# Expert rows fetched by row number, slot weights applied to results, and seven steps moved in a layer-stack kernel

## The reference

```
swiglu:  (silu(h @ w_gate) * (h @ w_up)) @ w_down          # ffn, w 1024x2816 and 2816x1024
mamba2:  y = ssd_chunked(...) + d_skip * xs ; g = y * silu(z)
         g = g * rsqrt(mean(g*g over a group of 256) + eps) * norm_w ; out = g @ w_out   # 8 groups
moe:     h = modulate(rms_norm(x), shift, scale)
         logits = h @ w_router + b ; a group of 4 experts is chosen, and two experts inside it
         out[t] = sum over 2 of weight[t, c] * (silu(h[t] @ w_gate[e]) * (h[t] @ w_up[e])) @ w_down[e]
         x = x + gate * out ; result = rms_norm(x) * norm_final
```

## Time and profile before

| | |
|---|---|
| median of 3 runs | 2996.58 us |
| the profiled execution | 2992.48 us, span 2991.2 us, mean granted TensorE clock 0.952 |
| PE (TensorE) busy | 2768.0 us, 93% |
| PEld (weight loads, beside PE) | 2222.6 us, 74% |
| DVE (VectorE) | 1613.2 us, 54% |
| ACT (ScalarE) | 727.7 us, 24% |
| POOL (GpSimd) | 775.2 us, 26% |
| DMA | 347.21 MB in 491364 packets, mean 116 GB/s |

### The profile page before, as it was taken

One profiled execution on the slowest core, in us unless ns is written; L12 is line 12 of the kernel. 1 busy time (PEld: TensorE's weight loads), 2 busy tenths in 40 slices (PEclk: granted clock), 3 DMA queues, 4 the chain that ended last, 5 costly groups with the idle time before them and its releaser, 6 DMA issues. The chain is left out here.

```text
span 2991.2 us, 32772 instructions
## 1 busy us (share of the span) xinstructions
PE 2768.0 (93%) x12795; PEld 2222.6 (74%) x12795; DVE 1613.2 (54%) x2319; ACT 727.7 (24%) x1336; POOL 775.2 (26%) x804
## 2 busy tenths in 40 slices
PE   5999999999899999999999699899999799858994
PEld 3888887777678888888888599788888576646663
DVE  3434468887743433564455366555454453445766
ACT  2101125555411001110011255210010343322323
POOL 1211121111112111221112288321112033133543
PEclk9999999999999999999999899999999896869997
DMA  3434432222133333354454200154444340149996
GB/s 105 144 112 137 130 92 71 67 68 64 50 87 97 97 94 99 92 148 136 118 147 132 63 1 1 53 147 138 120 141 92 45 63 15 35 141 314 380 377 228
DMA packets 491364, 347.21 MB, mean 116 GB/s; under 512 B 34430, under 2 KB 463307, under 8 KB 490955
## 3 DMA queue, kind: packets, MB, share of 16 engines
q1 hardware_dynamic: 451840, 270.05, 31.5%
q10 hardware_dynamic: 37066, 66.68, 6.4%
q0 software_dynamic: 2304, 8.39, 0.8%
HBM read 314.66 MB, written 30.41 MB: 115 GB/s over the span
## 5 line engine op out<-in xcount | busy, mean ns | idle before, releaser
L225 POOL TENSOR_SCALAR w_hi<-w_lo_exact 128x1024 fp32r<-128x1024 f32 x369 | 405.8, 1100 | 1798.9 <-DMA w_lo_exact<-in_ffn_w_gate 427.6
L240 PE MATMUL bank<-h_hi,w_hi 128*128 128x512 f32 x1992 | 795.9, 400 | 47.9 <-DVE h_lo L311 18.5
L241 PE MATMUL bank<-h_lo,w_hi 128*128 128x512 f32 x1992 | 782.4, 393 | 0.0
L242 PE MATMUL bank<-h_hi,w_lo 128*128 128x512 f32 x1992 | 781.8, 392 | 0.0
L232 DVE TENSOR_TENSOR w_lo<-w_lo_exact,w_hi 128x1024 fp32r<-128x1024 f32 x369 | 453.9, 1232 | 159.4 <-POOL w_hi L225 158.5
L240 PEld LDWEIGHTS bank<-h_hi,w_hi 128*128 128x128 f32 x1992 | 378.2, 190 | 144.5 <-issue 23.3
L242 PEld LDWEIGHTS bank<-h_hi,w_lo 128*128 128x128 f32 x1992 | 378.0, 190 | 80.7
L241 PEld LDWEIGHTS bank<-h_lo,w_hi 128*128 128x128 f32 x1992 | 378.5, 190 | 79.5 <-issue 3.6
L242 PE MATMUL bank<-g_hi,w_lo 128*128 128x512 f32 x704 | 280.9, 399 | 0.0
L241 PE MATMUL bank<-g_lo,w_hi 128*128 128x512 f32 x704 | 277.5, 394 | 0.0
L240 PE MATMUL bank<-g_hi,w_hi 128*128 128x512 f32 x704 | 276.1, 392 | 0.0
(11 more groups left out here) (458 smaller groups left out, 3742.7 us busy)
## 6 DMA issues: line engine op xcount, KB each, us to landing
w_lo_exact<-in_ffn_w_gate SPq DMA_DIRECT2D x88, 512.0 KB, 3.8
w_lo_exact<-in_ffn_w_up SPq DMA_DIRECT2D x88, 512.0 KB, 3.9
w_lo_exact<-in_ssm_w_in SPq DMA_DIRECT2D x48, 512.0 KB, 3.9
mod_w<-in_w_mod ACTq DMA_DIRECT2D x48, 512.0 KB, 3.8
e_lo_exact<-in_w_gate SPq DMA_DIRECT2D x92, 256.0 KB, 7.2
e_lo_exact<-in_w_up SPq DMA_DIRECT2D x92, 256.0 KB, 8.7
e_lo_exact<-in_w_down SPq DMA_DIRECT2D x46, 512.0 KB, 9.9
w_lo_exact<-in_ffn_w_down SPq DMA_DIRECT2D x32, 512.0 KB, 4.0
```

Of the source, the lines that this page charges most:

```text
L225: ge.tensor_scalar(k.w_hi[:, u % SLOTS, :], k.raw[:, u % SLOTS, :], 1.0, 0.0, ALU.mult, ALU.add).then_inc(*k.up("w hi", u))
L240: te.matmul(k.bank[bank][:, :], hi, x_hi, start=first, stop=False)
L241: te.matmul(k.bank[bank][:, :], hi, x_lo, start=False, stop=False)
L242: return te.matmul(k.bank[bank][:, :], lo, x_hi, start=False, stop=stop)
```

## The change

1. `rows_in` becomes an array of the 512 tokens' h rows, stored by four plain stores. The zero stores, the zero tile and the eight scatters go. For each of the 23 blocks a list of token numbers is computed: two one-hot tiles (`row_one`: the row within the block; `block_token`: the block, times the token's number) and eight matmuls. GpSimd gathers each block's rows by its list (`moe_rows_pool`), in place of the plain loads. An empty slot has token number 0.
2. The two weights of a token are brought to slots the same way (`slot_weight`) and multiplied in when `yo` is copied. At the end four gathers bring the first row of each token and four gathers that add bring the second; the two multiplications there go.
3. A gate/up unit holds rows 8p+2i and 8p+2i+1 of partition p: runs of 2 KB. The h columns are dealt to match when they are copied.
4. `norm_vector` scales tile n before it finishes tile n-1 (mixer and experts).
5. Expert stage's head: logits and the turning back of h run tile by tile as the norm makes them; GpSimd's first 12 splits wait for the norm's end; the loads of the router's bias and of the final norm come before the norm; `overflow_vector` comes after the lists.
6. The small loads of setup move to `ffn00`, half 1, j = 1.
7. In Mamba-2 the gate sum moves to unit s = 5 behind its sixth piece, and the last group's output blocks are dealt 8, 6, 2+2, 4, 2, and the rest.

```diff
-    for n in range(KD):
-        t = norm_slot(k, n)
-        ... scaled (n) ; wait h hi (n) ; h lo (n)
+    for n in range(KD + 1):
+        if n < KD:
+            ... scaled (n)
+        if n:
+            ve.wait_ge(*k.at("h hi", (stage, n - 1)))
+            ... h lo (n - 1)
@@ ffn_scalar
+            if (stage, half, j) == ("ffn00", 1, 1):
+                small_loads(k)
-            if stage == "ffn00":
-                zero_rows(k, half * HALF_FF + j)
@@ ssm_tensor
-            if s == 4 and g + 1 < GROUPS:
-                te.wait_ge(*k.at("gate added", g))
-                te.matmul(k.bank[3][:, :], k.ones[:, :], flat(k.lt[:, :, :]), ...)
+                for n in range(KD):
+                    ins = block(k, u, n, s % 2, k.h(n), n == 0, n == KD - 1)
+                    if s == 5 and n == 5:
+                        te.wait_ge(*k.at("gate added", g))
+                        te.matmul(k.bank[3][:, :], k.ones[:, :], flat(k.lt[:, :, :]), ...)
+LAST_GROUP_OUT = [(0, 0, 0, 8)], [(1, 0, 0, 6)], [(1, 0, 6, 8), (0, 1, 0, 2)], [(0, 1, 2, 6)], [(1, 1, 0, 2)]
@@ moe_load
-            se.dma_start(pair[:, :, c:c + D_EXPERT], w[0, expert, rows, :].rearrange("o (k p) m -> p (o k) m", p=P))
+            rows = w[0, expert, :, :].rearrange("o (p k) m -> p (o k) m", k=KD)[:, 2 * i:2 * i + 2, :]
+            se.dma_start(raw[:, c:c + 2 * D_EXPERT].rearrange("p (k m) -> p k m", k=2), rows)
@@ moe_pool
+    ge.wait_ge(*k.at("h lo", ("moe", KD - 1)))
     for n in range(RING):
         moe_split_pool(k, *UNITS_USED[n])
-    ge.wait_ge(*k.at("slots", "all"))
-    ge.wait_ge(*k.at("zeroed", "all"))
-    ge.wait_ge(*k.at("h natural", 2 * NT - 1))
-    for n in range(2 * NT):
-        ge.indirect_dma_start(k.rows_in[:, :], ...(k.slot_i[:, n:n + 1], 0), k.h_rows[:, n // 2, :], None)
+    ge.wait_ge(*k.at("placed", "rows"))
+    ge.wait_ge(*k.at("h stored", "all"))
+    for b in range(3):
+        moe_rows_pool(k, b)
     for n in range(RING, len(UNITS_USED)):
-        moe_split_pool(k, *UNITS_USED[n])
+        b, i = UNITS_USED[n]
+        if i == 2:
+            moe_rows_pool(k, b + 1)
+        moe_split_pool(k, b, i)
@@
-    for n in range(2 * NT):
-        ge.indirect_dma_start(k.picked[:, n, :], None, k.rows_out[:, :], ...(k.slot_i[:, n:n + 1], 0))
+    for c in range(2):
+        for tt in range(NT):
+            n = 2 * tt + c
+            if c:
+                ge.wait_ge(*k.at(f"picked {tt}", 0))
+            ge.indirect_dma_start(k.picked[:, 2 * tt, :], None, k.rows_out[:, :], ...(k.slot_i[:, n:n + 1], 0),
+                                  compute_op=ALU.add if c else ALU.bypass)
+def moe_rows_pool(k, b):
+    if b < BLOCKS:
+        if b >= 3:
+            k.ge.wait_ge(*k.at("rows turned", (b - 3, 1)))
+        k.ge.indirect_dma_start(k.rows[:, b % 3, :], None, k.rows_in[:, :], ...(k.list_i[:, PLACE_OF[b]:PLACE_OF[b] + 1], 0))
@@ moe_out_scalar
+        if b == 0 and half == 0:
+            ae.wait_ge(*k.at("placed", "weights"))
-        ae.copy(k.yo[...], k.bank[OUT_BANKS[half]][:, :])
+        ae.activation(k.yo[...], k.bank[OUT_BANKS[half]][:, :], ACT.Copy, scale=k.slot_weight[:, PLACE_OF[b]:PLACE_OF[b] + 1])
@@ moe_tensor, before the loop
+    for n in range(2 * NT):
+        ins = te.matmul(k.bank[HIDDEN_BANK][:, 0:BLOCKS + 1], k.row_one[:, n, :], k.block_token[:, n, :], ...)
+    for n in range(2 * NT):
+        ins = te.matmul(bank[:, 0:BLOCKS + 1], k.row_one[:, n, :].bitcast(F32), k.block_weight[:, n, :], ...)
+def lists_vector(k):
+    ... in_block_i = slot_i & 127 ; block_i = slot_i >> 7 ; block_f, in_block: copies to float
+    ... block_one = (0..23 == block_f)            # 128x192
+    ... block_token = block_one * token           # 128x192
+    ... row_one = (0..127 == in_block)            # 2 x 128x512
+    ve.wait_ge(*k.at("listed", "rows"))
+    ve.tensor_copy(k.list_i[:, :], k.bank[HIDDEN_BANK][:, 0:BLOCKS + 1])
+def slot_weights_vector(k):
+    ... block_weight = block_one * weight         # 128x192
+    ve.wait_ge(*k.at("listed", "weights"))
+    ve.tensor_copy(k.slot_weight[:, :], k.bank[SPARE_BANK][:, 0:BLOCKS + 1])
@@ moe_vector, moe_scalar, at the end
-        ae.activation(a, a, ACT.Copy, scale=k.weight[:, 0, tt:tt + 1])
-        ve.scalar_tensor_tensor(a, b, k.weight[:, 1, tt:tt + 1], a, ALU.mult, ALU.add)
```

More of the change, by code:

```diff
@@ L318, in norm_scalar @@
     for n in range(KD):
+        if between:
+            between(n)
         ae.wait_ge(*k.at("scaled", (stage, n)))
@@ L2543, in moe_tensor @@
     ins.then_inc(*k.up("ranked", 0))
-    te.wait_ge(*k.at("h natural", 2 * NT - 1))
+    te.wait_ge(*k.at("placed", "block token"))
+    for n in range(2 * NT):
+        te.wait_ge(*k.at("placed", ("row one", n // NT)))
+        ins = te.matmul(k.bank[HIDDEN_BANK][:, 0:BLOCKS + 1], k.row_one[:, n, :], k.block_token[:, n, :], start=n == 0, stop=n == 2 * NT - 1)
+    ins.then_inc(*k.up("listed", "rows"))
+    te.wait_ge(*k.at("placed", "block weight"))
+    for n in range(2 * NT):
+        ins = te.matmul(bank[:, 0:BLOCKS + 1], k.row_one[:, n, :].bitcast(F32), k.block_weight[:, n, :], start=n == 0, stop=n == 2 * NT - 1)
+    ins.then_inc(*k.up("listed", "weights"))
+    te.wait_ge(*k.at("h natural", (NT - 1, 1)))
     moe_turn_rows_tensor(k, 0)
@@ L2553, in moe_tensor @@
             n = b - 2
-            te.wait_ge(*(k.at("x natural", n - 1) if n else k.at("slots", "all")))
+            te.wait_ge(*(k.at("x natural", n - 1) if n else k.at("placed", "weights")))
             for m in range(n % 2 * 4, n % 2 * 4 + 4):
@@ L2617, in moe_scalar @@
     ae.preload_act_table(ACT.Silu)
-    ae.wait_ge(*k.at("scattered", "all"))
-    for b in range(3):
-        moe_rows_scalar(k, b)
     moe_rows_hi_scalar(k, 0)
@@ L2648, in moe_scalar, with natural_tile, moe_natural_scalar @@
     for tt in range(NT):
-        a, b = k.picked[:, 2 * tt, :], k.picked[:, 2 * tt + 1, :]
-        ae.wait_ge(*k.at(f"picked {tt}", 1))
-        ae.wait_ge(*k.at("choice", "weights"))
-        ae.activation(a, a, ACT.Copy, scale=k.weight[:, 0, tt:tt + 1]).then_inc(*k.up("combined a", tt))
-        if tt:
-            moe_last_scalar(k, tt - 1)
-    moe_last_scalar(k, NT - 1)
+        moe_last_scalar(k, tt)
+def natural_tile(k, i):
+    return (k.unit_at["moe"] + 1 + i) % NT
+def moe_natural_scalar(k, i, half):
+    tt = natural_tile(k, i)
+    k.ae.wait_ge(*k.at("h turned", (i, half)))
+    if i == NT - 1:
+        k.ae.wait_ge(*k.at("unit", k.unit_at["moe"]))
+    dealt = k.h_rows[:, tt, :].rearrange("p (k m a) -> p m k a", k=KD, m=KD)[:, half * 4:half * 4 + 4]
+    k.ae.copy(dealt, k.bank[NATURAL_BANKS[half][i]][:, :].rearrange("p (m a k) -> p m k a", m=4, k=KD)).then_inc(*k.up("h natural", (i, half)))
 def moe_last_scalar(k, tt):
```

187 lines of the change are left out of this document (119 added, 68 removed).

## The result

The changed kernel takes 2955.73 us (median of 4 runs, 2953.12 to 2961.22) against 3000.51 us for the kernel before beside it (4 runs, 2995.05 to 3011.38): ratio 0.9849, interval 0.9815 to 0.9882. 2952 us was forecast. The profiled execution has a span of 2951.9 us where the one before had 2991.2: 39.3 less, where 44.1 was forecast.

A forecast was written before the change was run, and what follows sets the result against it. TensorE, busy 2768.0 of 2991.2 us, bounds the kernel, so only its idle time or clock counts. Gains of 5.3 + 14 + 4.5 + 12.3 + 7 + 1 = 44.1 give 2948.4, forecast as 2952 us, range 2925 to 2980.

The forecast's parts named there:

- both halves: Setup: moving the small loads wins 15.0 us there and loses 9.7 where they go, net 5.3.
- 48.7 - 46.9: Mamba-2: group period falls from 48.7 to 46.9 us, VectorE's chain with ScalarE's answers; 1.7 times 7, 12 us gained.
- its 2.5: Mamba-2's last group: early output blocks cover waiting for the decay tile; 2.5 us gained, bounds 0 and 8.
- VectorE's 2 x 0.75 plus issue, 1.58, sets the pace: Mixer norm: with scales reordered VectorE takes 1.58 us a tile, before 2.43; 4.5 us gained, bounds 0 and 6.
- TensorE now does per tile 3.0 us, eight times 24 us: Expert stage's head: TensorE's work from 2634.9 puts the logits at 2658.7 against 2657.1.
- A clock of 1 here: Expert stage's head: full TensorE clock there, named as a sign that the prediction is wrong.
- moved behind the norm they cost nothing: Expert stage's head: GpSimd's 12 splits, 1.1 to 1.4 us each, are free there, the loop being over 30 us away.
- 16.0 were summed: Expert stage's head: slots at 2672.8, then lists, first gather and VectorE's longer queue; loop starts at about 2688.8.
- The 7 us of the 2 KB runs: Expert loop: 1024 fewer packets a block save 9 us over 21 blocks; 7 taken, bounds 12 and -10.
- 25 to 45 us beside its 118.2 busy of 256, not a bound: Expert loop: 20 gathers cost GpSimd 25 to 45 us of free time and do not lengthen the loop.
- rows late in the loop: Expert loop, slower rival: gathers landing later than about 15 us make every block wait, up to 3012 us; chance 0.09.
- 1 was forecast: End: plain and adding gathers finish near 2987.6 against 2988.5; 1 us gained, bounds -6 and +3.

The follow-up runs named there:

- Run 5: Changed kernel with d_skip loaded as 32 contiguous floats to each partition and dealt to dcol by two VectorE copies; 2949.0 us.
- run 7: Changed kernel without the wait that holds GpSimd's first 12 splits back to the norm's end; head 51.0 us against 51.8, route 5.8 against 9.8.
- runs 2 and 3: Changed kernel with loop gathers replaced by plain row loads from ScalarE's queue, 2947.1 us; the same plus 1 KB weight runs put back, 2957.2 us.
- Run 10: Changed kernel with the loop's 20 gathers replaced by plain loads of 128 consecutive rows issued from GpSimd; 2948.7 us, loop 251.4.
- run 12: Changed kernel with d_skip loaded wide, plain end gathers, slot weights after block 0's rows, loop gathers issued at unit (b, 4); 2934.8 us, 0.9794 of the kernel before.

## Why the prediction was right

The range and the sign held. The total (2952 against 2956) is closer than its terms, and that much is luck: +2.6 in the mixer's norm and +3.0 in the head met -6.3 in the loop and some -3 in Mamba-2.

- *Setup.* Right in both halves: 15.0 won, 7.54 plus the slow restart lost. Run 5 shows that the floats cause the loss. The 15.0 left with the floats and the zero stores together, and no run separates the two.
- *Mamba-2.* The mechanism was right: the wait goes and the chain of VectorE and ScalarE is next. The term "48.7 - 46.9" was mis-sized. The period went from 48.6 to 47.7, not to 46.9; VectorE waits more for ScalarE's answers than before (34.9 against 19.4), so the chain's own sum was too short. The piece with the last group gained 1.9 to 5.3 in the thirteen profiles, in the middle 3.0, where 4.2 was forecast; more than its 2.5 isn't shown.
- *Mixer norm.* The step "VectorE's 2 x 0.75 plus issue, 1.58, sets the pace" was right in kind and failed in size. Back to back on one engine two such instructions take 1.33 (scales at 2314.82, 2316.14, 2317.47), since each starts about 0.08 before the last one's recorded end. The pace before was read too long as well: from 2325.60 to 2342.60 there are seven tiles and one tile's way to `h_hi`; scale to scale it is 16.2 / 7 = 2.32, not 2.43. The eight scales now take 8.8 us from first to last instead of 16.2, and nearly all of it came through: 7.1 instead of 4.5.
- *Head.* "TensorE now does per tile 3.0 us, eight times 24 us" took the clock for given at 0.50. It rose at the third tile, and the logits came 5.2 earlier where 1.6 later was forecast. A clock of 1 here had been named as a sign of being wrong. The other way went the splits: "moved behind the norm they cost nothing" was wrong, they cost the route 4 (run 7). From `slot_i` on 17.6 were needed where 16.0 were summed.
- *Loop.* The 7 us of the 2 KB runs are there with plain rows (6.3, runs 2 and 3), and the gathers' 31.1 us on GpSimd lie inside the forecast 25 to 45. By the rule of the Trainium skill, "DMA: Bandwidth & Descriptors", section "SWDGE vs HWDGE vs iDMA", GpSimd can be locked out by VectorE while it writes the descriptors of its DMAs; 15 of the 19 gathers took over 1.7 us, each behind a subtraction. Run 10 doesn't bear out that reason: its plain loads are GpSimd's too and kept their 0.56 us beside the same subtractions. So what the long gathers wait for, and the plain loads don't, stays open. The failing step is "25 to 45 us beside its 118.2 busy of 256, not a bound": with gathers the loop took 255.4 us, with plain loads 249.6 and 251.4. GpSimd's busy share was no measure, and run 12 shows that the gathers' time in the queue alone is none either. GpSimd stands in a chain, load, split, split, `hid`, and TensorE's wait for `hid` goes with the loop's length. The rival "rows late in the loop" looked for the cost at the wrong place: the rows came in time (8.8).
- *End.* 0.5 where 1 was forecast, inside the spread of 1.4; the adding transfer's price, unknown then, is 0.6 us of issue and 1.9 until the result is taken.

## What to carry to other kernels

Ask of an issue moved to another engine not how busy that engine is, but what stands behind it in the queue and who waits for that. The gain of a faster transfer can go unseen, as here, when something else in the same change holds the loop. And many single floats in a small load were dear here beside the weights' loads: read them in rows and deal them out on chip. Before a stage's gain is believed, look how far the same stage varies between profiles of kernels in which it is untouched.

## What the runs showed of the hardware

- 2048 single floats held a 512 KB load of another queue back from 3.9 us to 21 in the changed kernel, and SyncE's later issue took 8.93 us instead of 0.37. Before, with the zero stores beside them, it was 23.5 us, and 14.84 for the issue. As 32 contiguous floats to each partition (run 5) they left no gap.
- A load by row number of 128 rows keeps GpSimd 0.95 to 0.97 us, or 1.75 to 1.95 when a subtraction of a split is running on VectorE as it begins (15 of 15 in the changed kernel's loop), ending 0.83 to 0.85 us after it. A plain load of the same size takes 0.55 to 0.60 either way (run 10).
- In the middle of the loop the sixteen DMA engines moved 378 GB/s with 1 KB runs and plain rows and 391 with 2 KB; with gathers 372 (1 KB) and 365 to 383 (2 KB), but 394 in run 12.
- TensorE's clock, half at the norm's start, was full from 2620.4 on, TensorE having worked without a gap since 2613.75. Before, with 0.6 to 1.4 us of waiting ahead of each tile's three matmuls, it stayed at half through the norm, and through the turning back behind it (17.59 busy of 20.30 us) as well.
